# Scan stage of a hybrid encoder: a pair of heads' products in the middle of the next slot, and the low parts of the weights on GpSimd

## The chip, the cores and the metric

One core of one Trainium2 chip runs the whole computation. Its engines are TensorE (PE; matmuls into PSUM, here the eight "banks"), VectorE (DVE), ScalarE (ACT), GpSimd (POOL, which works on SBUF only here) and SyncE (SP, which issues the loads of the weights). Each engine works through its own instructions in order; they wait for each other by semaphores. The metric is the device time of one execution in microseconds (us).

## What is computed

Two layers (DEPTH = 2) over a sequence of 512 positions and a width of 1024:

```python
for i in range(DEPTH):
    h = rmsnorm(x, norm1_g[i])
    u = h @ w_in[i]
    q, k, v, z, xbc, dt_raw, sc_b, sc_c, sc_x = jnp.split(u, split_at, axis=-1)
    a_out = attention_mixer(q, k, v, q_norm_g[i], k_norm_g[i], rel_table)
    s_out = ssd_mixer(z, xbc, dt_raw, ...)
    c_out = short_conv_mixer(sc_b, sc_c, sc_x, sc_conv_w[i], sc_conv_b[i])
    x = x + jnp.concatenate([a_out, s_out, c_out], axis=-1) @ w_out[i]
    x = x + conv_ffn(rmsnorm(x, norm2_g[i]), ffn_w_up[i], ...)
```

The part around the change is `ssd_mixer`: 16 heads in 2 groups, each scanned forward and backward in 4 chunks of 128 positions. For a head, with `cb` the products C x B of a chunk, masked by direction, and `a_cs` the running sums of dt*a:

```python
decay = jnp.exp(jnp.where(lower, seg, -jnp.inf))          # seg: differences of a_cs
y_diag = jnp.einsum('bclsge,bcsgep->bclgep', cb[..., None] * decay, X)
y_off = jnp.einsum('bclgn,bcgepn->bclgep', Cc, s_in) * jnp.exp(a_cs)[..., None]
y = y_fwd + y_bwd + d_skip * xs
y = y * silu(z); y = y * rsqrt(mean(y * y) + EPS); y = y * norm_g
```

All matrices are float32, and the output is float32.

## The kernel before

**Products in three parts.** Every large product is made of float32r halves: `products` (lines 1076 to 1080) multiplies high x high, high x low and low x high and adds them in one bank. A weight tile of 1024 rows x 128 columns ([128, 1024] in SBUF) is one "chunk" of the list CHUNKS. SP loads it into one of two buffers W (line 306, after the low part of the chunk two before, `w_lo`), ACT copies it to WHI (`w_high`, line 451, once the products of the chunk two before are done, `w_used`), and the low part WLO = W - WHI is made by POOL (`w_low`, line 359) in all stages but the scan stage, and by DVE (`low_after`, line 745) in the scan stage. The product of a chunk waits for its `w_lo`. Two chunks are in flight, so in the slot of chunk n the engines prepare chunk n + 2.

**Slots.** SLOTS (line 69) are the 28 chunks from the short convolution to the first half of the output product: 12 of the short convolution ("sc"), 8 of z, 8 of the output ("o1"). Called slots 0 to 27 here. TensorE does the 24 products of a slot's tile (`tile`, or `output_first` for "o1") and, beside them, the work of the scan. All five engines' programs are loops over the slots, written out by hand; the order of the instructions of an engine is the order in its loop. Which part stands in which slot comes from three tables: GROUP_AT = (2, 14) starts the two groups, ROWS_AT gives head h the slot GROUP_AT + 3 + h % 8 (5 to 12, and 17 to 24), PAIR_AT gives the pair of heads 2t and 2t + 1 a slot (7, 9, 11, 13 and 19, 21, 23, 25).

**A head** passes through the engines thus:

- TensorE, in the middle of the slot: `row_sums` (line 1239), two products, into banks 2 and 3. It waits for the head before to have been read (`seg_read`, and ACT's `ea_done`).
- DVE `seg` (lines 820 and 823): subtracts the columns' sums and limits the result, into one of three buffers (two in E, one in SQ).
- ACT: exponential of the row sums (line 604, EA), then of the buffer (line 607), and behind them in the same slot the high part of the next weights (`high_after`).
- DVE `weigh` (line 827): times the masked products CB. In the slot it stands behind `seg` and the eviction of the slot's tile. The low part of the weights stands behind `weigh`.
- POOL `add_directions` (line 389): adds the two directions (`gs_done`).

**A pair** t: TensorE, at the end of its slot, `from_states` (line 1265, 12 products, waits for DVE to have read the pair before, `y_read`) and `within` (line 1252, 16 products, waits for `gs_done` of both heads). DVE `combine` (lines 831, 838, 839), at the end of its slot's part: reads both, adds the forward half to XC. POOL `add_backward` (line 393) adds the other half, and later `gate` (line 398) multiplies with silu(z). DVE's eviction of a z tile (line 1004) of the second half waits for a gate (`y_comb`), because it writes over the z tile that the gate reads. After slot 27 POOL's `sum_squares(1)` (lines 372, 374) gives the sum for the second group's norm, which TensorE's `scan_sum(1)` (line 1120) takes behind the first output tile of the next stage ("o2").

**POOL's loop over the slots** has, in this order: the low part of the short convolution's product (line 414), `scale_states` (line 384), `add_directions`, `add_backward`, gates, and in slot 23 `sum_squares(0)`.

Of the kernel before, what the change touches and what calls it, by code (L numbers as in the profile page):

```python
# [103 lines left out]

GROUP_AT = (2, 14)
ROWS_AT = {GROUP_AT[h // 8] + 3 + h % 8: h for h in range(SSD_HEADS)}
PAIR_AT = {GROUP_AT[t // 4] + 5 + 2 * (t % 4): t for t in range(SSD_HEADS // 2)}


NORMS = ("norm1", "ssd0", "ssd1", "norm2")  # L110
# [24 lines left out]
def build_trunk(nc, a):  # L135
# [218 lines left out]
    def _(pool):  # L354
# [6 lines left out]
        def low_after(kind, i):  # L361

            n = now[0] * NCH + POS[kind, i] + 2
            if (kind, i) == ("o2", 0):
                pool.wait_ge(w_lo.handle, n)
            if n < DEPTH * NCH:
                w_low(n)

# [33 lines left out]
        for layer in range(DEPTH):  # L402
            now[0] = layer
            for pos in range(POS["sc", 0]):
                low_after(*CHUNKS[pos])
                if layer == 0 and CHUNKS[pos] == ("qk", 2):
                    pool.wait_ge(bias_row.handle, 2)
                    g.dma_start(scratch[:, :, :], rm["bias_row"][:, :].unsqueeze(1).to_broadcast([HEADS, COPIES, REL]))\
                        .then_inc(bias_stored.handle, 16)
            for s, (kind, i) in enumerate(SLOTS):  # L410
                if kind == "sc" and i % 3 == 2:
                    t = i // 3
                    pool.wait_ge(*sc_hi.at(t + 1))
                    g.tensor_tensor(rm["ml_sc"][:, t, :], SCP[:, :], rm["mh_sc"][:, t, :].bitcast(F32), ALU.subtract)\
                        .then_inc(sc_lo.handle, 1)
                for grp in range(SSD_GROUPS):
                    if 0 <= s - GROUP_AT[grp] < 3:
                        for j in range(2):
                            scale_states(6 * grp + 2 * (s - GROUP_AT[grp]) + j)
                if s in ROWS_AT:  # L420
                    add_directions(ROWS_AT[s])
                if s in PAIR_AT:
                    add_backward(PAIR_AT[s])
                if s in (16, 17):
                    gate(2 * (s - 16))
                    gate(2 * (s - 16) + 1)
                if s in (20, 22, 24):
                    gate(s // 2 - 6)
                if s == 25:
                    gate(7)  # L430
                if s == 23:
                    sum_squares(0)
            sum_squares(1)
            for m in range(KT):
                low_after("o2", m)
            for j in range(2 * FF_T):
                low_after("up", j)
                if j % 2 == 1:
                    t = j // 2
                    pool.wait_ge(*ff_hi.at(t + 1))  # L440
                    g.tensor_tensor(FLO[:, t, :], FP[:, :], FHI[:, t, :].bitcast(F32), ALU.subtract).then_inc(ff_lo.handle, 1)  # L441
            for i in range(DOWN_C * KT):
                low_after("dn", i)
# [259 lines left out]
    def _(dve):  # L703
# [33 lines left out]
            v.scalar_tensor_tensor(mixed("l", 8 + t), XC[:, t, :], par(PA_SNG + t), mixed("h", 8 + t).bitcast(F32),  # L737
                                   ALU.mult, ALU.subtract).then_inc(y_lo.handle, 1)

        def low_after(kind, i):  # L740

            n = now[0] * NCH + POS[kind, i] + 2
            dve.wait_ge(w_hi.handle, n + 1)
            dve.wait_ge(w_lo.handle, n)
            v.tensor_tensor(WLO[:, n % 2, :], W[:, n % 2, :], WHI[:, n % 2, :].bitcast(F32), ALU.subtract).then_inc(w_lo.handle, 1)  # L745

        def root_ready(name):
            dve.wait_ge(*root_done.at(NORMS.index(name) + 1))

# [113 lines left out]
        for layer in range(DEPTH):  # L863
# [77 lines left out]
            for s, (kind, i) in enumerate(SLOTS):  # L941
# [10 lines left out]
                    dve.sem_inc(cs_col.handle, 1)  # L952
                if s in ROWS_AT:
                    seg(ROWS_AT[s])
                for grp in range(SSD_GROUPS):
                    if s == GROUP_AT[grp] + 1:
                        mask_products(grp)
                    if 0 <= s - GROUP_AT[grp] - 1 < 3:
                        for j in range(2):
                            state_in(6 * grp + 2 * (s - GROUP_AT[grp] - 1) + j)  # L960
# [23 lines left out]
                    v.tensor_tensor(X[:, i, :], bank(b), X[:, i, :], ALU.add).then_inc(evac[b].handle, 1)  # L984
                if s in ROWS_AT:
                    weigh(ROWS_AT[s])
                low_after(kind, i)
                if s in PAIR_AT:
                    combine(PAIR_AT[s])
                if kind == "sc" and i % 3 == 1:  # L990
                    t = i // 3
# [75 lines left out]
    def _(pe):  # L1067
# [32 lines left out]
            if k == KT - 1:  # L1100
                ins.then_inc(w_used.handle, 1)

        def tile(kind, i, width=P, head=None):

            for k in range(KT):
                if k == KT // 2 and head is not None:
                    row_sums(head)
                block_of(kind, i, k, width)

        def norm_sum(norm):  # L1110
# [155 lines left out]
                             start=True, stop=True)  # L1266
            ins.then_inc(yo_mm.handle, 1)

        def output_first(m, head):

            s, b = weights("o1", m), tile_bank("o1", m)
            for k in range(KT):
                if k == KT // 2 and head is not None:
                    row_sums(head)
                at = slice(P * k, P * k + P)
                ins = products(bank(b), WHI[:, s, at], WLO[:, s, at], mixed("h", k), mixed("l", k), k == 0, k == KT - 1)
            ins.then_inc(w_used.handle, 1)
# [14 lines left out]
        for layer in range(DEPTH):  # L1292
# [47 lines left out]

            for s, (kind, i) in enumerate(SLOTS):
                if kind == "o1":
                    output_first(i, ROWS_AT.get(s))
                else:
                    tile(kind, i, head=ROWS_AT.get(s))
                if s == 0:
                    pv(PAIRS - 1)
                    cumulate()
# [5 lines left out]
                for grp in range(SSD_GROUPS):  # L1354
# [4 lines left out]
                    if 0 <= s - GROUP_AT[grp] - 1 < 3:  # L1359
                        for j in range(2):  # L1360
                            chunk_state(6 * grp + 2 * (s - GROUP_AT[grp] - 1) + j)
                if s in PAIR_AT:
                    from_states(PAIR_AT[s])
                    within(PAIR_AT[s])
                if s == 26:
# [125 lines left out]
```

## Time and profile before

| | us |
|---|---|
| median of 3 runs (lowest to highest) | 1684.43 (1684.07 to 1684.91) |
| the profiled execution's own time | 1689.05 |
| its span, first to last instruction | 1687.2 |

| engine | busy us | share of the span |
|---|---|---|
| TensorE matmul | 1649.8 | 98% |
| TensorE weight load | 1306.7 | 77% |
| DVE | 1003.6 | 59% |
| ACT | 679.4 | 40% |
| POOL | 723.3 | 43% |

The granted TensorE clock is 0.997 of full speed. The scan stage of layer 0 lies at about 212 to 431 us, that of layer 1 at about 1046 to 1266 us; in the 40 equal slices of the span (42 us each) DVE is at 7 to 9 tenths there and TensorE at 9. By line, the chain that ended last runs 71% through lines 1078 to 1080 (the three products), 3% through line 745, 1% through line 820. The page's group of line 359 (POOL's low part) has 202 instructions with 490.4 us, that of line 745 (DVE's) 56 with 78.0 us.

How to read it: a row of the timeline gives an instruction's start, its length and, in brackets, how long its engine had been idle and which instruction ended that. The length of an instruction of DVE or POOL is from its start to its end, whatever it waited for inside the engine. A TensorE product is shown with its whole latency (0.39 us and more) though the next starts 0.23 us later.

### The profile page before, as it was taken

How to read it: one execution, taken by the hardware profiler on the slowest of the kernel's cores; microseconds unless marked ns; L12 is line 12 of the kernel's file. 1: busy time of each engine (PE TensorE's matmuls, PEld its weight loads, DVE VectorE, ACT ScalarE, POOL GpSimd, SP SyncE). 2: the span in 40 equal slices, each digit the busy share in tenths (PEclk: the TensorE clock that was granted, in tenths of full speed). 3: DMA queues.
4: the chain of work that ended last, by engine and by line, in shares of the span. 5: the costliest groups of instructions: out<-in, count | busy, mean ns of one | idle time of the engine just before them, and what ended most of it. 6: DMA issues, size and time to landing. Idle time of an engine off the chain costs nothing.

```text
span 1687.2 us, 20176 instructions
## 1 busy us (share of the span) xinstructions
PE 1649.8 (98%) x7876; PEld 1306.7 (77%) x7876; DVE 1003.6 (59%) x1387; ACT 679.4 (40%) x932; POOL 723.3 (43%) x355
## 2 busy tenths in 40 slices
PE   7999999998999999999999999999989999999999
PEld 5777777777778888888877777777777788888887
DVE  5589859778774555422236898596787654545100
ACT  5445553344443333322244555433543433333221
POOL 3432224345445555554444222243454455555443
PEclk9999999999999999999999999999999999999999
DMA  5532111212223232222224221122112223222223
GB/s 167 136 90 81 53 63 63 76 63 76 75 88 100 88 100 91 98 91 94 93 86 124 85 73 64 63 65 73 63 63 91 94 91 100 88 100 89 93 100 106
DMA packets 43230, 147.32 MB, mean 87 GB/s; under 512 B 5152, under 2 KB 5920, under 8 KB 43136
## 3 DMA queue, kind: packets, MB, share of 16 engines
q1 hardware_dynamic: 42752, 145.28, 26.6%
q0 software_dynamic: 384, 0.75, 0.4%
q8 instruction: 63, 1.03, 0.3%
q14 instruction: 31, 0.25, 0.1%
HBM read 143.17 MB, written 2.85 MB: 87 GB/s over the span
## 4 chain that ended last, share of the span: by engine, by line
PE 80%; DVE 10%; issue 4%; ACT 3%; POOL 2%; DMA 1%; SPq 0%; DVEq 0%; ACTq 0%; POOLq 0%
PE banks L1078 24%; PE banks L1080 23%; PE banks L1079 23%; DVE sb_w_lo L745 3%; PE banks L1170 2%; PE banks L1149 2%; PE banks L1158 2%; DVE sb_e L820 1%; ACT sb_exp_cs L604 1%; PE banks L1225 1%; PE banks L1129 1%; DVE sb_t_normed L838 1%; ACT sb_e L607 1%; DVE sb_sc_acc L995 1%; POOL sb_sq_ssd L372 1%
## 5 line engine op out<-in xcount | busy, mean ns | idle before, releaser
L359 POOL TENSOR_TENSOR sb_w_lo<-sb_w_raw,sb_w_hi 128x1024 fp32r<-128x1024 f32 x202 | 490.4, 2428 | 632.3 <-ACT sb_w_hi L451 632.3
L1078 PE MATMUL banks<-sb_h_hi,sb_w_hi 128*128 128x512 f32 x1360 | 559.1, 411 | 16.1 <-POOL sb_w_lo L359 10.8
L451 ACT ACTIVATE sb_w_hi<-sb_w_raw 128x1024 fp32r<-128x1024 f32 x258 | 272.3, 1057 | 674.4 <-PE banks L1080 668.1
L1080 PE MATMUL banks<-sb_h_hi,sb_w_lo 128*128 128x512 f32 x1360 | 538.2, 396 | 0.0
L1079 PE MATMUL banks<-sb_h_lo,sb_w_hi 128*128 128x512 f32 x1360 | 538.1, 396 | 0.0
L1078 PEld LDWEIGHTS banks<-sb_h_hi,sb_w_hi 128*128 128x128 f32 x1360 | 257.2, 189 | 100.0 <-issue 35.9
L1079 PEld LDWEIGHTS banks<-sb_h_lo,sb_w_hi 128*128 128x128 f32 x1360 | 257.4, 189 | 61.7 <-issue 6.9
L1080 PEld LDWEIGHTS banks<-sb_h_hi,sb_w_lo 128*128 128x128 f32 x1360 | 257.1, 189 | 59.7
L1043 DVE TENSOR_TENSOR banks<-banks,sb_rstd 128x512 f32<-128x512 f32 x88 | 61.5, 699 | 144.1 <-PE banks L1080 135.7
L1079 PE MATMUL banks<-sb_ff_lo,sb_w_hi 128*128 128x512 f32 x352 | 139.0, 395 | 0.0
L1080 PE MATMUL banks<-sb_ff_hi,sb_w_lo 128*128 128x512 f32 x352 | 139.0, 395 | 0.0
L1078 PE MATMUL banks<-sb_ff_hi,sb_w_hi 128*128 128x512 f32 x352 | 139.0, 395 | 0.0
L1058 DVE TENSOR_TENSOR sb_x_stream<-banks,sb_x_stream 128x512 f32<-128x512 f32 x16 | 11.1, 692 | 199.2 <-PE banks L1080 199.2
L745 DVE TENSOR_TENSOR sb_w_lo<-sb_w_raw,sb_w_hi 128x1024 fp32r<-128x1024 f32 x56 | 78.0, 1392 | 23.4 <-ACT sb_w_hi L451 23.4
L604 ACT ACTIVATE sb_exp_cs<-banks 64x768 f32<-64x768 f32 x32 | 25.8, 807 | 143.9 <-DVE sb_e L820 113.0
L441 POOL TENSOR_TENSOR sb_ff_lo<-sb_ff_prod,sb_ff_hi 128x512 fp32r<-128x512 f32 x44 | 57.0, 1295 | 51.4 <-DVE sb_ff_hi L1054 51.4
L389 POOL TENSOR_TENSOR sb_e<-sb_e 128x512 f32<-128x512 f32 x24 | 51.4, 2142 | 63.6 <-DVE sb_e L827 63.6
L1078 PEld LDWEIGHTS banks<-sb_ff_hi,sb_w_hi 128*128 128x128 f32 x352 | 66.4, 189 | 15.5
L1079 PEld LDWEIGHTS banks<-sb_ff_lo,sb_w_hi 128*128 128x128 f32 x352 | 66.4, 189 | 15.4
L1080 PEld LDWEIGHTS banks<-sb_ff_hi,sb_w_lo 128*128 128x128 f32 x352 | 66.4, 189 | 15.3
L768 DVE SCALAR_TENSOR_TENSOR sb_xc<-banks,sb_params,sb_xc 128x509 f32<-128x509 f32 (+2 forms) x96 | 71.9, 749 | 4.5 <-ACT sb_xc L508 1.7
L514 ACT ACTIVATE sb_probs<-sb_scores,sb_neg_max 128x512 f32<-128x512 f32 x64 | 45.7, 716 | 57.3 <-DVE sb_neg_max L794 57.3
(199 smaller groups left out, 2321.1 us busy)
## 6 DMA issues: line engine op xcount, KB each, us to landing
sb_w_raw<-w_in SPq DMA_DIRECT2D x88, 512.0 KB, 3.4
sb_w_raw<-w_up SPq DMA_DIRECT2D x88, 512.0 KB, 3.3
sb_w_raw<-w_out SPq DMA_DIRECT2D x32, 512.0 KB, 3.4
sb_w_raw<-w_down SPq DMA_DIRECT2D x32, 512.0 KB, 3.4
sb_bias_t<-bias_rows SPq DMA_DIRECT2D x16, 448.0 KB, 5.7
sb_w_raw<-w_down SPq DMA_DIRECT2D x16, 384.0 KB, 3.0
sb_x_stream<-x_t SPq DMA_DIRECT2D x4, 512.0 KB, 6.3
out_t<-sb_x_stream SPq DMA_DIRECT2D x8, 256.0 KB, 3.9
```

The costliest lines, as they stand in the source:

```text
L359: g.tensor_tensor(WLO[:, n % 2, :], W[:, n % 2, :], WHI[:, n % 2, :].bitcast(F32), ALU.subtract).then_inc(w_lo.handle, 1)
L389: g.tensor_tensor(head_e(h)[:, 0, :], head_e(h)[:, 0, :], head_e(h)[:, 1, :], ALU.add).then_inc(gs_done.handle, 1)
L441: g.tensor_tensor(FLO[:, t, :], FP[:, :], FHI[:, t, :].bitcast(F32), ALU.subtract).then_inc(ff_lo.handle, 1)
L451: sc.activation(WHI[:, n % 2, :], W[:, n % 2, :], ACT.Copy).then_inc(w_hi.handle, 1)
L514: sc.activation(PR[:, u % 4, :], S[:, u % 2, :], ACT.Exp, bias=NEGMAX[:, u % 4:u % 4 + 1], scale=-1.0, accum_out=DEN[:, u % 4:u % 4 + 1]). ...
L604: sc.activation(EA[half, (h // 2) % 2, :, :].rearrange("p d l -> p (d l)"), BANK[half, 2:4, :].rearrange("p b s -> p (b s)")[:, P:P + 768] ...
L745: v.tensor_tensor(WLO[:, n % 2, :], W[:, n % 2, :], WHI[:, n % 2, :].bitcast(F32), ALU.subtract).then_inc(w_lo.handle, 1)
L768: ins = v.scalar_tensor_tensor(acc[:, lo:hi], src[:, lo + o:hi + o], par(PA_CONV7 + 8 * n + t), acc[:, lo:hi], ALU.mult, ALU.add)
L1043: v.tensor_tensor(bank(b), bank(b), RSTD, ALU.mult).then_inc(up_scaled.handle, 1)
L1078: mm(out, whi, hhi, start=start, stop=False)
L1079: mm(out, whi, hlo, start=False, stop=False)
L1080: return mm(out, wlo, hhi, start=False, stop=stop)
```

## The change

It has two parts.

**Pairs.** PAIR_AT becomes GROUP_AT + 6, 8, 10 and 11: slots 8, 10, 12, 13 and 20, 22, 24, 25. Of each four, the first three pairs' `from_states` and `within` stand in the middle of the slot's tile, ahead of that slot's `row_sums` (new function `between`); the fourth stays at the end of its slot. DVE's `combine` of the first three moves up, behind `seg` and ahead of the tile's eviction and `weigh`. POOL's `add_backward` follows PAIR_AT.

**Low parts.** DVE's `low_after` goes; POOL makes the 28 low parts of the stage too, as the first thing in each slot, ahead of line 414, `scale_states`, `add_directions`, `add_backward` and the gates. POOL's wait for DVE's last low part, at ("o2", 0), goes.

```diff
-PAIR_AT = {GROUP_AT[t // 4] + 5 + 2 * (t % 4): t for t in range(SSD_HEADS // 2)}
+PAIR_AT = {GROUP_AT[t // 4] + 6 + 2 * (t % 4) - (t % 4 == 3): t for t in range(SSD_HEADS // 2)}
 ...
 # POOL
             n = now[0] * NCH + POS[kind, i] + 2
-            if (kind, i) == ("o2", 0):
-                pool.wait_ge(w_lo.handle, n)
             if n < DEPTH * NCH:
                 w_low(n)
 ...
             for s, (kind, i) in enumerate(SLOTS):
+                low_after(kind, i)
                 if kind == "sc" and i % 3 == 2:
 ...
 # DVE
-        def low_after(kind, i):
-
-            n = now[0] * NCH + POS[kind, i] + 2
-            dve.wait_ge(w_hi.handle, n + 1)
-            dve.wait_ge(w_lo.handle, n)
-            v.tensor_tensor(WLO[:, n % 2, :], W[:, n % 2, :], WHI[:, n % 2, :].bitcast(F32), ALU.subtract).then_inc(w_lo.handle, 1)
 ...
                 if s in ROWS_AT:
                     seg(ROWS_AT[s])
+                if s in PAIR_AT and PAIR_AT[s] % 4 < 3:
+                    combine(PAIR_AT[s])
 ...
                 if s in ROWS_AT:
                     weigh(ROWS_AT[s])
-                low_after(kind, i)
-                if s in PAIR_AT:
+                if s in PAIR_AT and PAIR_AT[s] % 4 == 3:
                     combine(PAIR_AT[s])
 ...
 # TensorE
-        def tile(kind, i, width=P, head=None):
+        def between(s):
+
+            if s in PAIR_AT and PAIR_AT[s] % 4 < 3:
+                from_states(PAIR_AT[s])
+                within(PAIR_AT[s])
+            if s in ROWS_AT:
+                row_sums(ROWS_AT[s])
+
+        def tile(kind, i, width=P, slot=None):
 
             for k in range(KT):
-                if k == KT // 2 and head is not None:
-                    row_sums(head)
+                if k == KT // 2 and slot is not None:
+                    between(slot)
                 block_of(kind, i, k, width)
 ...
-                if s in PAIR_AT:
+                if s in PAIR_AT and PAIR_AT[s] % 4 == 3:
                     from_states(PAIR_AT[s])
                     within(PAIR_AT[s])
```

`output_first` takes the slot in the same way.

## Rows read from the trace of the kernel before

**Rows 1.** Timeline, TensorE, layer 0's scan stage: start us, us, engine, line, what, [idle before <-releaser]

```profile
267.17 0.50 PE L1078 MATMUL banks<-sb_h_hi,sb_w_hi 128*128 128x512 f32 x1 [0.88 <-DVE sb_w_lo L745]
...
290.75 0.32 PE L1252 MATMUL banks<-sb_squares,sb_x_tok 128*64 128x128 f32 x1 [1.31 <-POOL sb_e L389]
...
321.52 1.09 PE L1252 MATMUL banks<-sb_e,sb_x_tok 128*64 128x128 f32 x16 [1.82 <-POOL sb_e L389]
...
383.07 0.50 PE L1078 MATMUL banks<-sb_mh_at,sb_w_hi 128*128 128x512 f32 x1 [0.19 <-DVE sb_w_lo L745]
...
394.15 0.73 PE L1239 MATMUL banks<-sb_cs,sb_selectors 128*128 128x512 f32 x2 [1.98 <-ACT sb_exp_cs L604]
...
416.14 1.67 PE L1252 MATMUL banks<-sb_e,sb_x_tok 128*64 128x128 f32 x16 [2.96 <-POOL sb_e L389]
...
437.37 1.13 PE L1120 MATMUL banks<-sb_sq_ssd,sb_constants 128*128 128x512 f32 x2 [0.77 <-POOL sb_sq_ssd L374]
```

**Rows 2.** Busy time by engine, columns: us, PE busy (x), PEld, DVE, ACT, POOL, PEclk, DMA share, GB/s

```profile
244.00:424.00 180.00, 170.87 (x858) 135.82 (x857) 146.34 (x169) 70.90 (x79) 78.78 (x47) 0.99 0.21 68
```

**Rows 3.** Timeline, DVE and POOL side by side (columns as in rows 1)

```profile
456.40 2.40 POOL L359 TENSOR_TENSOR sb_w_lo<-sb_w_raw,sb_w_hi 128x1024 fp32r<-128x1024 f32 x1 [2.99 <-ACT sb_w_hi L451]
...
456.60 2.76 DVE L1025 TENSOR_TENSOR sb_x_stream<-sb_x_stream,sb_t_normed 128x512 f32<-128x512 f32 x1
...
408.54 2.39 POOL L372 TENSOR_TENSOR sb_sq_ssd<-sb_sq_ssd 128x1024 f32<-128x1024 f32 x1
...
408.87 2.61 DVE L823 TENSOR_SCALAR sb_e<-sb_e 128x1024 f32<-128x1024 f32 x1
...
286.13 1.22 DVE L827 TENSOR_TENSOR sb_e<-sb_e,sb_cb 128x1024 f32<-128x1024 f32 x1
...
286.30 2.19 POOL L414 TENSOR_TENSOR sb_ml_sc<-sb_sc_prod,sb_mh_sc 128x512 fp32r<-128x512 f32 x1 [4.41 <-DVE sb_mh_sc L981]
...
287.27 2.31 DVE L745 TENSOR_TENSOR sb_w_lo<-sb_w_raw,sb_w_hi 128x1024 fp32r<-128x1024 f32 x1
...
358.19 1.22 DVE L820 TENSOR_TENSOR sb_e<-banks,sb_small 128x1024 f32<-128x1024 f32 x1
...
358.79 1.29 POOL L398 TENSOR_TENSOR sb_xc<-sb_xc,sb_z 128x512 f32<-128x512 f32 x1
```

**Rows 4.** One line's instructions: count, ns min/median/max, first and last start, form

```profile
L359 POOL TENSOR_TENSOR sb_w_lo<-sb_w_raw,sb_w_hi x202: 2343/2403/3075, 7.6 to 1675.4; 128x1024 fp32r<-128x1024 f32 x101
...
L745 DVE TENSOR_TENSOR sb_w_lo<-sb_w_raw,sb_w_hi x56: 1214/1220/2323, 224.6 to 1268.0; 128x1024 fp32r<-128x1024 f32 x56
...
L389 POOL TENSOR_TENSOR sb_e<-sb_e x24: 1295/2212/2282, 266.0 to 1249.8; 128x512 f32<-128x512 f32 x24
...
L823 DVE TENSOR_SCALAR sb_e<-sb_e x24: 693/694/2614, 258.6 to 1244.8; 128x1024 f32<-128x1024 f32 x24
...
L995 DVE SCALAR_TENSOR_TENSOR sb_sc_acc<-sb_sc_cx,sb_params,sb_sc_acc x16: 744/752/1784, 234.0 to 1138.9; 128x511 f32<-128x511 f32 x16
...
L1025 DVE TENSOR_TENSOR sb_x_stream<-sb_x_stream,sb_t_normed x32: 691/693/2759, 434.7 to 1315.1; 128x512 f32<-128x512 f32 x32
```

**Rows 5.** Timeline, TensorE and ACT, slots 19 to 22 of layer 0

```profile
365.73 1.50 PE L1265 MATMUL banks<-sb_bc,sb_s_in 128*128 128x128 f32 x12
...
368.19 0.50 PE L1078 MATMUL banks<-sb_mh_at,sb_w_hi 128*128 128x512 f32 x1
...
376.18 1.28 ACT L612 ACT_TABLE_LOAD   x1
...
380.70 1.06 ACT L451 ACTIVATE sb_w_hi<-sb_w_raw 128x1024 fp32r<-128x1024 f32 x1
```

**Rows 6.** Timeline, ACT and POOL, before the second scan sum

```profile
431.05 1.06 ACT L451 ACTIVATE sb_w_hi<-sb_w_raw 128x1024 fp32r<-128x1024 f32 x1 [1.81 <-PE banks L1080]
...
435.71 1.60 POOL L374 TENSOR_TENSOR sb_sq_ssd<-sb_sq_ssd 128x512 f32<-128x512 f32 x1
```

**Rows 7.** DMA issues: count, KB each, median us to landing

```profile
sb_w_raw<-w_out SPq DMA_DIRECT2D x32, 512.0 KB, 3.4
```

More of the change, by code:

```diff
@@ L1267, in from_states, with output_first @@
             ins.then_inc(yo_mm.handle, 1)
-        def output_first(m, head):
+        def output_first(m, slot):
             s, b = weights("o1", m), tile_bank("o1", m)
             for k in range(KT):
-                if k == KT // 2 and head is not None:
-                    row_sums(head)
+                if k == KT // 2:
+                    between(slot)
                 at = slice(P * k, P * k + P)
@@ L1342, in _ @@
                 if kind == "o1":
-                    output_first(i, ROWS_AT.get(s))
+                    output_first(i, s)
                 else:
-                    tile(kind, i, head=ROWS_AT.get(s))
+                    tile(kind, i, slot=s)
                 if s == 0:
```

## The prediction

> **What bounds the kernel now.** I read the page's busy shares first: TensorE (PE) is busy for 98% of the span, so only its waits and its work can move the time. Then its waits in layer 0's scan stage, which the change rewrites. The timeline says where they fall and who ends them: POOL's sum of the directions (L389), ACT's exponential of the sums (L604), DVE's low part of a weight tile (L745), POOL's tree of squares (L374) [rows 1]. Call the tiles of SLOTS slots 0 to 27. A plain slot is 24 products of 0.232 us, 5.57 us; one with a head's row sums 6.04; one that also has a pair's products (2.46, from 365.73 to 368.19 [rows 5], and a slower start behind them) 8.58. The idle times are 0.9 (low part, before slot 7), 1.3 (slot 9), 1.8 (13), 0.2 (22), 2.0 (23), 3.0 (25) and 0.8 (second scan sum), 9.9 together; counted from one slot's start to the next, with the slow restart behind each wait, it is 11.8 us a layer. Layer 1 repeats it. So 24 us is the most that better order can give. Behind all these waits stands DVE: in 244 to 424 us it is busy 146 of 180 us, POOL 79 [rows 2].
>
> **What decides: the path into SBUF that DVE and POOL share.** In the output stage POOL's low part starts at 456.40 and takes 2.40; DVE's L1025, normally 0.69, starts at 456.60 and takes 2.76: it ends 0.7 after POOL does. At 408.54 the same happens to L823 (2.61 for 0.69), which has one SBUF input. The other way round, at 286.13 DVE's L827 runs 1.22, POOL's L414 behind it takes 2.19, and DVE's next, L745, waits for that and takes 2.31: each holds the path for its whole instruction, the one that asked first goes next. An instruction of DVE that reads a bank is not held up: L820 at 358.19 takes 1.22 under POOL's L398 from 358.79 [rows 3]. So POOL's L389, whose median is 2.21, is really some 1.2 (its shortest is 1.295) and spends the rest behind L745 [rows 4].
>
> **The parts and their prices.**
> Low parts (28 a layer) leave DVE: L745 takes 1.22 undisturbed, so DVE is relieved of 28 x 1.22 = 34 us a layer. They come to POOL at 2.40 each (L359 median), 67 us a layer onto an engine that has time for it: 79 of 180 busy becomes some 135, less about 15 for L389 and L414 that no longer queue behind L745 [rows 2, 4]. What is not free is the path. For two slots with one pair (6.04 + 8.58 = 14.6 us) its users are, before: DVE 2 x (0.69 L823 + 1.22 L827 + 1.22 L745) + 0.56 L839 = 6.8; POOL 2 x 1.2 L389 + 1.0 L393 + 1.3 L398 = 4.7; 11.5, 79%. After: DVE 4.4, POOL 2 x 2.4 + 4.7 = 9.5; 13.9, 95%. In the short-convolution slots L995 (twice 0.75) and L981 (0.43) come once in three slots and add 1.3, and L414 (1.1) takes L398's place: 15.0, over 100% [rows 3, 4]. (0.56, 1.0 and 0.43 are the shortest of L839, L393 and L981 in the same view as rows 4.) DVE and POOL work in order and wait on each other within a slot, so a path at 95% must cost waits.
>
> Where they land I get by carrying the clocks of the queues forward slot by slot, with these durations and that rule for the path. Done for the kernel before, as a check, it returns waits of 0.9, 0.3 (slot 8's row sums, not in the rows), 1.5, 2.0, 0.4, 2.4, 3.6, 0.4 in the order above and a small 0.3 at slot 13's start: 11.8. For the changed kernel, layer 0:
> - Slots 4 to 7. The high part for slot 6 ends at 251.9, POOL holds the path to 254.3, and DVE's L858, which ran at 252.36, now goes at 254.3. DVE is 2 us late, saves 1.2 of L745, and is late again by POOL's L414 and L389 ahead of head 1's L823. L827 follows that head's exponential, then the low part for slot 8 takes 2.4 and ends at 274.4 where TensorE is ready at 272.5: **1.9**. But the 0.9 before slot 7 is gone, since that low part no longer waits for L827 and L414.
> - Slots 10 to 13: the same chain (seg, POOL's hold, exponential, high part, 2.4) gives 0.6 at slot 11, 1.8 at slot 13. `within` waits 1.1 for L389 at the end of slot 13 (2.0 before). The 1.5 of pair 1 goes: its `within` now comes at 293.3 in the middle of slot 10, and head 3's sum is ready at 292.8.
> - Slots 16 to 19: the gates (L398) now stand behind a low part, so Z's eviction and with it the bank come late: 0.9.
> - Slots 20 to 25: low parts 1.1 (slot 20), 2.2 (22), 0.9 (24), 0.8 (25). The 2.2 can be followed alone. Pair 4's products (2.46: 365.73 to 368.19) now precede head 11's row sums in slot 20, which end 2.88 + 2.46 + 0.62 = 5.96 into it. Then L820 1.22, L823 0.73, L607 1.06, Silu with its two table loads 4.52 (376.18 to 380.70), L451 1.06, L359 2.40: 16.9, against 6.04 + 8.58 = 14.62 until slot 22 [rows 4, 5]. Head 13's wait (2.4) goes, since pair 5's reading, which L604 needed first, no longer stands between.
> - Slot 25: pair 7 stays at the end, but pair 6 now stands in slot 24, so `from_states` waits 1.7 for its reading, and `within` 3.3 for L389: 5.0 for 3.6.
> - Second scan sum: the low parts of slots 26 and 27 now stand ahead of `sum_squares(1)` on POOL. High part 431.05 + 1.06, low 2.40, L372 2.39, L374 1.6: 438.5, for 437.3 before [rows 1, 3, 6]. By the stepping 1.6 for 0.4.
> Sum after: 1.9 + 0.6 + 1.8 + 1.1 + 0.9 + 1.1 + 2.2 + 0.9 + 0.8 + 5.0 + 1.6 = 17.9, less 11.8: about 6 a layer. With every duration moved by up to 5% and the comparison repeated, the middle is 5.4 and eight in ten lie within 2.3 to 8.8. I take 5.4, **11 us for two layers**.
>
> Small parts. Fewer changes of kind on TensorE: six pairs a layer now adjoin row sums. A row-sum slot costs 6.04 = 24 x 0.232 + 0.47, its two products and no more, so I take nothing; at most 0.1 each, 1.2 us in all, as a gain. SP's loads wait for low parts (`w_lo`): at worst a low part ends when its slot starts; the load lands 3.4 later, and the high part waits for the slot's end, 5.57 later [rows 7]. That cover of 2.2 holds. The wait for `w_lo` that went from ("o2", 0) was satisfied by order anyway: nothing. The moved `combine` issues the same four instructions; behind it on DVE stand the tile's eviction and `weigh`, which the stepping holds. One bound has no row: whether a low part of POOL in these slots is slowed by something else. Its longest anywhere is 3.08 (median 2.40); at 2.6 throughout the stepping gives 9.7 a layer, 19 in all; if it found the path always free, -8 a layer.
>
> The Trainium skill ("Perfetto Trace Analysis", Optimizing Scalar/DVE Operations) says that since the two engines share an SBUF port, moving operations between them might not help. By it the sum would be 0 and the time 1684; by the rows it is neither 0 nor all loss, because DVE's reads of banks do run beside POOL [rows 3]. It speaks for the third rival.
>
> **Rivals.**
> 1. It works as drawn: POOL's low parts fall under DVE's bank reads (L820, L831, L838 and the evictions, about 5.5 us in two slots) and DVE's lead removes the waits. Without any hold of the path the stepping leaves only slot 22 (2.2) and the second scan sum (1.6) of 11.8: 8 a layer, 1668. For it: POOL has the time, TensorE's 6 us waits for L389 are what the edit aims at. Against: the holds of [rows 3]. It decides if POOL's holds cost DVE less than half of the 34 us of relief; the stepping has them grow from 14 to 38 us a layer, which eats 24. A half of it, -4 a layer, gives 1676.
> 2. POOL becomes the pacer: low parts take 2.6 or more among DVE's holds, `add_directions` and the gates slip, and pair products wait in mid-slot. 9 to 10 a layer: 1703. For: 95% of the path. Against: L359's mean is 2.43.
> 3. Gains and losses cancel: the hold of L858 in slot 4 falls otherwise, DVE keeps its lead, and slots 8, 11 and 13 don't wait (1.9 + 0.6 + 1.8 = 4.3 of the 5.4 a layer): 2 us in all, 1686. For: which engine asks first there is a matter of 0.5 us. Against: other tenths then put the same hold elsewhere, as the moved durations showed.
>
> **From this to the numbers.** The profiled execution took 1689.05 (span 1687.2), 4.6 over the median of 1684.43; the 11 us are read from it and added to the median: 1695. Chances: forecast (up 4 to 17) 0.54, rival 1 0.20, rival 2 0.13, rival 3 0.13. Within 0.2%, 3.4 us, is about what can't be told from no change. Faster 0.21, same 0.14, slower 0.65. Range 1677 to 1705: it leaves out the full form of rival 1 and the tail of rival 2. The likeliest case's own range is 1688 to 1702.
>
> **What would show it.** Right: TensorE's waits name L359 POOL as releaser of L1078 in both scan stages, some 2 us ahead of slots 8, 13 and 22; L823, L827, L858 and L995 have means well above 0.69, 1.22, 0.69 and 0.75; L389 falls from 2.2 towards 1.3; the second scan sum waits about 2 us. The waits of L1252 in slot 9 and L1239 in slot 23 are gone in any case. Wrong: no such waits of L1078, with L823 and L827 at their old lengths; then DVE's relief came through and the time is under 1680. Over 1702 with L359 above 2.6 is rival 2.

## The result and the profile after

The changed kernel takes 1701.7 us (median of four runs, 1699.0 to 1703.7), the kernel before 1684.7 on the same chip: a ratio of 1.0093, 95% interval 1.0080 to 1.0105. It is slower by 17 us; the forecast was 1695, 11 slower. The profiled execution of the changed kernel took 1699.0, that of before 1689.1, so the pair of traces holds 9.9 us of the difference.

The page of the changed kernel begins:

```profile
span 1697.1 us, 20118 instructions
PE 1652.9 (97%) x7876; PEld 1306.1 (77%) x7876; DVE 990.5 (58%) x1331; ACT 680.8 (40%) x932; POOL 834.2 (49%) x411
L359 POOL TENSOR_TENSOR sb_w_lo<-sb_w_raw,sb_w_hi 128x1024 fp32r<-128x1024 f32 x258 | 630.2, 2443 | 784.5 <-ACT sb_w_hi L450 784.5
```

DVE has lost 56 instructions and only 13.1 us of busy time (1003.6 before); the group that left it, in the page of before:

```profile
L745 DVE TENSOR_TENSOR sb_w_lo<-sb_w_raw,sb_w_hi 128x1024 fp32r<-128x1024 f32 x56 | 78.0, 1392 | 23.4 <-ACT sb_w_hi L451 23.4
```

The 56 low parts took 78.0 us of DVE. So 65 of these 78 came back as longer instructions of DVE's that remain. That is the first reading that matters: a busy time counts the waiting for the path too, and 140 us of new work on POOL (L359: 630.2 for 490.4) made DVE's other work 65 us longer. POOL's own busy time rose by 111 only, because its other instructions, L389 above all, no longer wait behind DVE's low part.

In the window of [rows 2] (us, busy PE, PEld, DVE, ACT, POOL, then granted clock, DMA share, GB/s) POOL is at 119 us, DVE at 136:

```profile
244.00:424.00 180.00, 168.71 (x845) 133.25 (x844) 136.10 (x143) 69.68 (x76) 119.23 (x68) 0.99 0.19 65
```

TensorE's waits in layer 0's scan stage, which answer to [rows 1] (the timeline; start us, us, engine, line, what, idle before and its releaser; L1071 is L1078 of before, L1253 is L1252, L1121 is L1120):

```profile
273.99 0.50 PE L1071 MATMUL banks<-sb_h_hi,sb_w_hi 128*128 128x512 f32 x1 [1.82 <-POOL sb_w_lo L359]
...
312.89 0.50 PE L1071 MATMUL banks<-sb_h_hi,sb_w_hi 128*128 128x512 f32 x1 [0.71 <-POOL sb_w_lo L359]
...
320.96 1.09 PE L1253 MATMUL banks<-sb_e,sb_x_tok 128*64 128x128 f32 x16 [0.89 <-POOL sb_e L387]
...
360.55 0.47 PE L1071 MATMUL banks<-sb_h_hi,sb_w_hi 128*128 128x512 f32 x1 [1.24 <-DVE sb_z L997]
...
367.61 0.50 PE L1071 MATMUL banks<-sb_mh_at,sb_w_hi 128*128 128x512 f32 x1 [0.78 <-POOL sb_w_lo L359]
...
384.95 0.70 PE L1071 MATMUL banks<-sb_mh_at,sb_w_hi 128*128 128x512 f32 x1 [2.44 <-POOL sb_w_lo L359]
...
416.02 1.58 PE L1266 MATMUL banks<-sb_bc,sb_s_in 128*128 128x128 f32 x12 [0.43 <-DVE sb_xc L831]
...
420.57 1.09 PE L1253 MATMUL banks<-sb_e,sb_x_tok 128*64 128x128 f32 x16 [2.98 <-POOL sb_e L387]
...
441.51 1.12 PE L1121 MATMUL banks<-sb_sq_ssd,sb_constants 128*128 128x512 f32 x2 [2.07 <-POOL sb_sq_ssd L372]
```

They sum to 13.4 us for 9.9 before (idle time alone, without the slow start behind a wait). The waits of slots 7, 9 and 23 are gone, and the low parts that POOL makes now end four waits of L1071: in slots 8, 13, 20 and 22. Layer 1 shows the same list within 0.05. TensorE's products are all there in both, so the new order costs these waits and what follows a wait (below).

How POOL's low part holds DVE, from the timeline of DVE and POOL side by side, slot 4 and slot 25 (columns as above):

```profile
251.78 2.40 POOL L359 TENSOR_TENSOR sb_w_lo<-sb_w_raw,sb_w_hi 128x1024 fp32r<-128x1024 f32 x1 [3.36 <-ACT sb_w_hi L450]
252.19 2.54 DVE L850 TENSOR_TENSOR sb_t_normed<-sb_s_in,sb_decays 128x512 f32<-128x512 f32 x1
...
415.56 2.53 POOL L359 TENSOR_TENSOR sb_w_lo<-sb_w_raw,sb_w_hi 128x1024 fp32r<-128x1024 f32 x1 [0.96 <-ACT sb_w_hi L450]
416.40 2.78 DVE L819 TENSOR_TENSOR sb_e<-sb_e,sb_cb 128x1024 f32<-128x1024 f32 x1
```

The instruction of 0.68 (L850) takes 2.54, that of 1.22 (L819) takes 2.78. The first ends 0.55 after POOL does, the second 1.09: each a little less than its own undisturbed length, as if it had begun its work only when POOL was through. The groups by line (count, busy time, mean ns of one, idle before) give the same over both layers:

```profile
L815 DVE TENSOR_SCALAR sb_e<-sb_e 128x1024 f32<-128x1024 f32 x24 | 31.9, 1330 | 0.8
L819 DVE TENSOR_TENSOR sb_e<-sb_e,sb_cb 128x1024 f32<-128x1024 f32 x24 | 40.4, 1685 | 6.5 <-ACT sb_e L606 6.5
L850 DVE TENSOR_TENSOR sb_t_normed<-sb_s_in,sb_decays 128x512 f32<-128x512 f32 x16 | 16.6, 1037 | 0.0
L387 POOL TENSOR_TENSOR sb_e<-sb_e 128x512 f32<-128x512 f32 x24 | 36.3, 1511 | 7.0 <-DVE sb_e L819 7.0
```

Their means before were 896 (L823), 1223 (L827), 774 (L858) and 2142 (L389).

**What the prediction did not have: TensorE's clock.** Windows of 5 us of the changed kernel, with the same columns:

```profile
385.00:390.00 5.00, 5.00 (x18) 4.05 (x19) 4.43 (x5) 2.66 (x3) 4.18 (x3) 0.66 0.33 108
1225.00:1230.00 5.00, 5.00 (x30) 4.21 (x30) 3.58 (x5) 3.94 (x5) 3.95 (x4) 0.68 0.24 94
```

The first begins where the wait of 2.44 ahead of slot 22 ends. The products there:

```profile
385.45 0.63 PE L1072 MATMUL banks<-sb_ml_at,sb_w_hi 128*128 128x512 f32 x1
...
388.01 0.62 PE L1072 MATMUL banks<-sb_ml_at,sb_w_hi 128*128 128x512 f32 x1
388.43 0.43 PE L1073 MATMUL banks<-sb_mh_at,sb_w_lo 128*128 128x512 f32 x1
388.70 0.40 PE L1071 MATMUL banks<-sb_mh_at,sb_w_hi 128*128 128x512 f32 x1
...
395.21 0.40 PE L1071 MATMUL banks<-sb_mh_at,sb_w_hi 128*128 128x512 f32 x1
```

They start every 0.43 us for some three microseconds and every 0.23 after that: the lower of the clock's two levels (1.2 GHz), then the upper (2.4 GHz). The slot lasts 395.21 - 384.95 = 10.26. The kernel before falls too, behind its own longest wait (the 2.96 of [rows 1]):

```profile
415.00:420.00 5.00, 3.86 (x22) 3.10 (x23) 4.19 (x6) 0.00 (x0) 3.29 (x2) 0.66 0.65 208
```

A wait does not always bring it: behind the 2.98 in slot 25 of layer 0 the changed kernel kept its clock, behind the 2.97 of layer 1 it did not. Over the scan stages the profiled execution of before has three such falls (behind 1.82 and twice 2.96), that of the changed kernel four (slot 22 in both layers, slot 25 and the second scan sum in layer 1). In the scan stages of all fourteen traces each fall follows a wait of 1.8 us or more, and several waits of that length are followed by none.

### The profile page after: what moved, and what is told of

Its sections match the earlier page's. It is cut to its first block, busy times and chain, and to the rows that moved or that the text cites. A ratio compares the mean times of both kernels' runs of the same rounds, so it can differ in the third digit from the quotient of the medians.

```text
span 1697.1 us, 20118 instructions
## 1 busy us (share of the span) xinstructions
PE 1652.9 (97%) x7876; PEld 1306.1 (77%) x7876; DVE 990.5 (58%) x1331; ACT 680.8 (40%) x932; POOL 834.2 (49%) x411
## 4 chain that ended last, share of the span: by engine, by line
PE 81%; DVE 9%; issue 5%; POOL 3%; ACT 2%; DMA 0%; SPq 0%; DVEq 0%; POOLq 0%; ACTq 0%
PE banks L1071 24%; PE banks L1072 24%; PE banks L1073 24%; PE banks L1171 2%; PE banks L1150 2%; PE banks L1159 2%; DVE sb_e L812 1%; POOL sb_w_lo L359 1%; DVE sb_e L815 1%; DVE sb_e L819 1%; ACT sb_w_hi L450 1%; PE banks L1130 1%; PE banks L1253 1%; DVE sb_t_normed L850 1%; POOL sb_squares L382 1%
## 5 line engine op out<-in xcount | busy, mean ns | idle before, releaser
L359 POOL TENSOR_TENSOR sb_w_lo<-sb_w_raw,sb_w_hi 128x1024 fp32r<-128x1024 f32 x258 | 630.2, 2443 | 784.5 <-ACT sb_w_hi L450 784.5
L1071 PE MATMUL banks<-sb_h_hi,sb_w_hi 128*128 128x512 f32 x1360 | 557.7, 410 | 21.1 <-POOL sb_w_lo L359 14.9
L1071 PEld LDWEIGHTS banks<-sb_h_hi,sb_w_hi 128*128 128x128 f32 x1360 | 256.4, 189 | 105.9 <-issue 38.3
L1071 PE MATMUL banks<-sb_ff_hi,sb_w_hi 128*128 128x512 f32 x352 | 138.9, 395 | 0.0
L1071 PEld LDWEIGHTS banks<-sb_ff_hi,sb_w_hi 128*128 128x128 f32 x352 | 66.3, 188 | 15.6
L1038 DVE SCALAR_TENSOR_TENSOR sb_ff_val<-banks,sb_params,sb_ff_val 128x511 f32<-128x511 f32 x44 | 33.0, 750 | 46.2 <-ACT sb_ff_val L683 46.2
L1038 DVE SCALAR_TENSOR_TENSOR sb_ff_gate<-banks,sb_params,sb_ff_gate 128x511 f32<-128x511 f32 x44 | 33.0, 750 | 45.8 <-ACT sb_ff_gate L683 45.8
```

The lines of the kernel that those rows point to most:

```text
L359: g.tensor_tensor(WLO[:, n % 2, :], W[:, n % 2, :], WHI[:, n % 2, :].bitcast(F32), ALU.subtract).then_inc(w_lo.handle, 1)
L1038: step(v.scalar_tensor_tensor(acc[:, 1:SEQ], BANK[:, b, 0:SEQ - 1], par(col), acc[:, 1:SEQ], ALU.mult, ALU.add))
L1071: mm(out, whi, hhi, start=start, stop=False)
```

## The experiments

Three questions: is it POOL's hold of the path that costs; how much of the relief of DVE is left when the hold is shorter or better placed; and are the falls of the clock the part that the order of the queues does not explain?

**The pairs moved, nothing else.** The low parts stay on DVE behind `weigh` (and POOL's wait for them comes back). Comments in the code below are added here.

```
+POOL_LOW = ()
-                low_after(kind, i)              # POOL, at the slot's start
+                if s in POOL_LOW:
+                    low_after(kind, i)
...
+                if s not in POOL_LOW:           # DVE, behind weigh
+                    low_after(kind, i)
```

> Pairs moved as in the changed kernel, but all 28 low parts of the scan stage stay on DVE, behind weigh. Theory 1 (the path into SBUF that DVE and POOL share): the pairs' move is worth nothing by itself; the queues carried forward give +0.3 us a layer, so 1685 +- 3, with TensorE's waits at low parts before slots 10 (2.4) and 22 (2.1) in place of slots 9 and 23. Theory 2 (the order: the pair in mid-slot delays the row sums and with them the slot): most of the loss stays, 1697 to 1702.

1686.3 for 1686.4 of the kernel before: ratio 1.0001 (0.9991 to 1.0011). Waits of TensorE in 240 to 450 us (us in total, times, longest):

```profile
PE banks L1084 <- DVE sb_w_lo L748: 4.9, 3, 2.1
PE banks L1266 <- POOL sb_e L390: 2.8, 2, 2.3
```

The waits for the sum of the directions shrink, those for DVE's low part take their place. The pairs' half of the change is worth nothing alone.

**The low parts moved, nothing else.** They are on POOL at the slot's start as in the change, and the pairs stay at the ends of slots.

> Low parts on POOL at the start of each slot as in the changed kernel, pairs at the end of slots 7, 9, 11, 13 as before. Theory 1: worse than the changed kernel, since within now comes before POOL has added the directions: +8.9 us a layer, 1702 and, with the clock's dips behind long waits, up to 1710; waits at L1252 of 2 to 3 us in slots 7, 9, 21. Theory 2 (order of the pairs is the loss): the low parts on POOL alone are a gain or nothing, 1675 to 1685.

1706.9: ratio 1.0119 (1.0105 to 1.0133), 20 us slower than before.

```profile
PE banks L1243 <- POOL sb_e L387: 12.1, 6, 3.8
```

The whole loss is in this half: on POOL the low part now stands ahead of the sum of the directions, and a pair at the end of its slot waits for that six times (3.8 us at worst). Moving the pairs takes 3 to 4 us of it back (20.4 to 17.0, though the intervals of their ratios just touch), as they have half a slot more to spare.

**Shorter holds.** POOL makes 512, then 16, of the 1024 columns of each low part in these slots; the rest of the low part is left out, and nothing else changes.

```
-                low_after(kind, i)
+                low_after(kind, i, 512)      # and 16 in the second kernel
```

> The changed kernel, but POOL makes only columns 0 to 511 of each of the 28 low parts of the scan stage (the other half of WLO keeps old values). Each low part then takes about 1.25 us and holds the path as long as DVE's did. Theory 1: the loss turns into a gain, -8.3 us a layer against before, 1668 +- 4. Theory 3 (POOL's place in the order, behind the end of the slot, is what hurts, not the length of its holds): still slower than before, 1690 or more.

> The changed kernel, but POOL makes only 16 of the 1024 columns of each of the 28 low parts of the scan stage (the rest of WLO keeps old values). DVE keeps its full relief of 34 us a layer, POOL holds the path for almost nothing. Theory 1 (path): all waits go but some 0.7 us at slot 25: -11.2 us a layer, 1662 +- 4. Theory 3 (POOL's place in the order): no better than the half lows, 1670.

With 512 columns 1670.5, ratio 0.9903 (0.9890 to 0.9917). With 16 columns 1666.2, ratio 0.9883 (0.9869 to 0.9896). All of TensorE's waits in layer 0's stage with 512 columns:

```profile
PE banks L1071 <- POOL sb_w_lo L359: 1.3, 1, 1.3
PE banks L1121 <- POOL sb_sq_ssd L372: 1.0, 1, 1.0
PE banks L1253 <- POOL sb_e L387: 0.9, 1, 0.9
```

The second is 0.2 us outside what was expected (1662 +- 4). So the relief of DVE, with the pairs moved, is worth 19 us, and half of POOL's work per slot still leaves 16 of it. It is the second 512 columns that cost, 31 us against 4 for the first; some 6 of the 31 are falls of the clock in the changed kernel, which these two, with no wait over 1.3 us in this stage, do not have. This says nothing of *how* POOL's work costs, by its own length or by the hold. The next run shows what holds alone do.

**The hold alone.** To the kernel with the pairs moved, one operation of POOL's is added in each slot from 2 on, on tiles of its own; nobody waits for its result. DVE still makes the low parts.

```
+                if s >= 2:
+                    pool.wait_ge(w_hi.handle, now[0] * NCH + POS[kind, i] + 3)
...
+                    g.tensor_tensor(SM[:, 1:4, :], CON[:, 0:6, :]..., CON[:, 1:7, :]..., ALU.subtract)...
```

> The kernel with the pairs moved and all low parts on DVE, and in each slot from 2 on one more instruction on POOL at the place of the low part, behind the same wait, that subtracts 768 columns of the constants into dead storage: nobody waits for its result, it only holds the path for 1.8 us and delays what stands behind it on POOL. Theory 1: slower by 20 to 28 us a layer than the pairs alone (DVE has not been relieved here), 1727 to 1742. If holds were harmless and only the low part's later end hurt, 1686 to 1690.

1743.5 (1740.6 to 1746.0), ratio 1.0339 (1.0318 to 1.0359). The low parts on DVE and the added group, then what TensorE waits for in 240 to 450 us:

```profile
L753 DVE TENSOR_TENSOR sb_w_lo<-sb_w_raw,sb_w_hi 128x1024 fp32r<-128x1024 f32 x56 | 102.7, 1833 | 18.0 <-ACT sb_w_hi L459 18.0
...
L418 POOL TENSOR_TENSOR sb_small<-sb_constants 128x768 f32<-128x768 f32 x52 | 107.6, 2069 | 200.1 <-ACT sb_w_hi L459 200.1
```

```profile
PE banks L1089 <- DVE sb_w_lo L753: 15.4, 7, 4.1
PE banks L1271 <- POOL sb_e L391: 6.6, 2, 3.3
PE banks L1089 <- DVE sb_z L1015: 3.4, 3, 2.4
```

Fifty-two operations of 2.07 us that produce nothing that is used cost 57 us, 1.1 each. DVE issues the same instructions as with the pairs alone, and its busy time goes from 1011.5 to 1062.5 us; its low part takes 1833 ns in the mean for 1422, and TensorE's waits for DVE's tiles (L753, L1015) go from 4.9 us to 18.8 in this stage. Not all of the 57 is the path's: POOL's queue is longer too (6.6 us for L391, for 2.8), DVE waits for POOL in places, and the profiled execution has ten falls of the clock in the scan stages where the pairs alone had none, at most 20 us by the clocks of its windows (an estimate). The time is just above what was expected (1727 to 1742). How the loss of the changed kernel divides between the holds and the low part's own 2.40 us on POOL (for 1.22 on DVE) no run shows. By the prediction's own working the waits at slot 22 and at the second scan sum come from the low part's length and place and would be there without any hold.

**Low parts put by slot.** First the twelve slots in which the stepping found POOL's low part cheapest (0, 2, 3, 5, 6, 8 to 11, 13, 14, 22), the rest on DVE; and a kernel that gives DVE back only the last two, 26 and 27.

> The changed kernel's pairs; low parts on POOL in slots 0, 2, 3, 5, 6, 8 to 11, 13, 14, 22 and on DVE in the other 16, chosen by carrying the queues forward. Theory 1: -3.8 us a layer, 1677, and a little less if fewer long waits also mean fewer dips of the granted clock; waits left at slots 13 (1.3), 22 (2.0), 25 (3.9). If the path were not what decides, the mix would lie between e1 and the changed kernel, 1690 or more.

> The changed kernel with the low parts of slots 26 and 27 back on DVE, so that sum_squares(1) no longer stands behind them on POOL. The queues carried forward give 1.2 us a layer less than the changed kernel, the wait at the second scan sum 0.4 to 0.8 us as before in place of 2.1. With no wait of over 2 us there, no fall of the granted clock behind it either: 1702 - 2.4 - up to 3, so 1697 to 1699. If the clock's falls are unrelated to waits, 1699 to 1700.

1678.7 for the first, ratio 0.9950 (0.9937 to 0.9964). 1697.4 for the second, ratio 1.0068 (1.0055 to 1.0081), 4 us under the changed kernel, though the two intervals just touch. The wait of the second scan sum goes from 2.1 to 0.8 in both layers, and no fall follows it. With the falls taken out (how, is shown in the next section) its trace gives 1694.2 for the changed kernel's 1696.0, so the two low parts themselves cost some 2 us and the rest is falls.

Then each slot got the place that the stepping liked best, and so did the pairs: 0, 1, 2, 5 and 6 in mid-slot, 3, 4 and 7 at the end of slots 13, 19 and 25.

```
+MID = (0, 1, 2, 5, 6)
+LOW_BY = 'PPDPDPPDPPEPDQEPEDPPDEEQDDPE'
```

P is POOL at the slot's start, Q POOL behind the sum of the directions, D DVE behind `weigh`, E DVE ahead of it. The string has 14 on POOL and 14 on DVE; the expectation counts 13 and 15.

> A better order, searched by carrying the queues forward: pairs 0, 1, 2, 5, 6 in mid-slot, 3, 4, 7 at the end of slots 13, 19, 25; low parts on POOL in 13 slots (two of them behind add_directions) and on DVE in 15 (six of them ahead of weigh). -5.7 us a layer: 1673, 3 to 4 us under the mixed kernel; waits left at slots 22 (1.5), 25 (1.9 and 1.1), none over 2 us, so few falls of the clock.

1673.2 (1672.8 to 1674.0), ratio 0.9925 (0.9913 to 0.9938): some 12 us faster than the kernel before, 28 faster than the changed one, the best that computes all of the low parts. What is left in layer 0's stage:

```profile
PE banks L1089 <- POOL sb_w_lo L361: 1.7, 2, 1.1
PE banks L1089 <- DVE sb_w_lo L751: 1.3, 1, 1.3
PE banks L1139 <- POOL sb_sq_ssd L376: 0.8, 1, 0.8
PE banks L1271 <- POOL sb_e L391: 0.6, 1, 0.6
```

No wait is over 1.3, and the granted clock of its whole span was 1.000 in all its runs.

**Filling the waits, to keep the clock up.** Three products of constants with ones (nobody reads the result; 2.7 us of TensorE; a row counts each as two) go into four waits of the changed kernel: ahead of `within` of pairs 3 and 7, at the end of slot 21, and ahead of the second scan sum. The same goes into the kernel before.

```
+                if s == 21:
+                    warm(7)          # 3 products, 128x512, fp32, into a bank that is free
```

> The changed kernel, with three products more of the constants (about 2 us of TensorE, into a bank that is overwritten next) ahead of four long waits of each layer: within of pairs 3 and 7, the start of slot 22, the second scan sum. They fill idle time; the waits end when they ended. Theory A (the granted clock falls to 1.2 GHz for some 2.8 us behind a long wait, and that costs 1.4 us each time): no falls are left there, 4 to 7 us less than the changed kernel, 1695 to 1698. Theory B (the falls have nothing to do with the waits): same as the changed kernel or slower by what of the extra products isn't hidden (up to 1 us each at pair 3 and the second scan sum), 1700 to 1706.

> The kernel before, filled in the same way ahead of within of pairs 3 and 7 and of the second scan sum (its longest waits are 3.0, 1.8 and 0.8 us; three products take about 2). Theory A: no falls behind slots 13 and 25, so up to 2.8 us less in the executions that had them, less 0.2 to 1.2 us where the extra products outlast the wait: 1683 to 1686 with a smaller spread than before's 1684.4 to 1691. Theory B: slower by 2 to 3 us, the same spread.

1702.4 for the changed kernel, ratio 1.0091 (1.0074 to 1.0107), no change; 1690.6 for before, ratio 1.0022 (1.0012 to 1.0031), slower, with a spread of 3.9 us for 7.3. By time neither speaks for the clock. The traces do. In the scan stages each has two falls left, and all four stand behind a wait that was not filled: slot 8's 1.8 in the changed kernel (windows from 270 and 1115 us), slot 23's 2.0 in the kernel before (395 and 1235 us). At slot 22 of the first:

```profile
385.65 2.74 PE L1198 MATMUL banks<-sb_constants 128*128 128x512 f32 x6
...
388.27 0.51 PE L1071 MATMUL banks<-sb_mh_at,sb_w_hi 128*128 128x512 f32 x1
...
396.97 0.39 PE L1071 MATMUL banks<-sb_mh_at,sb_w_hi 128*128 128x512 f32 x1
```

The slot takes 8.70 for 10.26. But 2.7 us of filling outlasts three of the four waits (0.9, 2.4, 2.1), and in the kernel before those of 1.8 and 0.8, and gives the gain back: before's runs with a mean clock of 1.000 took 1684.1 to 1684.4, those filled 1689.6 to 1689.7, and the fillings outlast their waits by 2.8 us a layer. So the last pair: fillings that fit (one product of 0.9 us at the end of slot 7; two at the end of slot 21, ahead of `within` 7 and ahead of the second scan sum), and the changed kernel once more on the same chip.

> The changed kernel with fewer extra products, each set shorter than the wait that it fills (one product is 0.9 us): one at the end of slot 7 (wait 1.8), two at the end of slot 21 (2.4), two ahead of within of pair 7 (3.0), two ahead of the second scan sum (2.1). None of them moves the end of a wait. Theory A (falls of the granted clock behind the waits are part of the loss): clock near 1.000, 1692 to 1696, against 1699 to 1704 for the changed kernel on the same chip. Theory B (they are not): as the changed kernel, 1699 to 1704.

> The changed kernel itself, on the chip of the run beside it: 1699 to 1704 with clocks of 0.993 to 0.997, the longer the lower the clock.

Fitted: 1696.4 (1695.6 to 1697.4 in six runs), ratio 1.0056 (1.0043 to 1.0069). The changed kernel again: 1704.9 (1698.8 to 1705.3), ratio 1.0099 (1.0082 to 1.0116). From `within` of slot 25 to the second scan sum, first fitted, then the changed kernel again:

```profile
421.21 1.09 PE L1264 MATMUL banks<-sb_e,sb_x_tok 128*64 128x128 f32 x16 [1.25 <-POOL sb_e L387]
...
442.17 1.12 PE L1124 MATMUL banks<-sb_sq_ssd,sb_constants 128*128 128x512 f32 x2 [0.37 <-POOL sb_sq_ssd L372]
```

```profile
422.23 1.98 PE L1253 MATMUL banks<-sb_e,sb_x_tok 128*64 128x128 f32 x16 [2.97 <-POOL sb_e L387]
...
446.06 1.13 PE L1121 MATMUL banks<-sb_sq_ssd,sb_constants 128*128 128x512 f32 x2 [2.07 <-POOL sb_sq_ssd L372]
```

The stretch takes 20.96 and 23.83, with granted clocks of 1.00 and 0.67 in 420 to 425 us: this fall costs 2.9. Not every fall costs. Slot 22 and `from_states` of slot 25 in the fitted kernel, where slot 22 did not fall:

```profile
385.56 0.50 PE L1071 MATMUL banks<-sb_mh_at,sb_w_hi 128*128 128x512 f32 x1 [0.74 <-POOL sb_w_lo L359]
...
416.66 1.58 PE L1277 MATMUL banks<-sb_bc,sb_s_in 128*128 128x128 f32 x12 [1.28 <-DVE sb_xc L831]
```

That is 31.10 us, and 31.07 (384.95 to 416.02) in the changed kernel, whose slot 22 did fall: `from_states` waits for DVE there (1.28, and 0.43 behind the fall), so the fall in slot 22 makes later waits shorter and costs nothing. Layer 1 has 31.10 and 31.11.

Seven products a layer, 12.6 us of *added* work on TensorE, make the kernel 8.4 us faster, and the spread shrinks from 6.5 to 1.7. No queue of another engine was touched. The times are 0.4 and 0.9 us above what was expected. The mean clock of the whole span was 1.000 in all six runs with fillings, 0.992 to 0.996 in those without; in those five the time goes with it (0.996: 1698.8; 0.993: 1704.3; 0.992: 1704.9 to 1705.3). So the falls of the clock are a real part of the loss, and what differs from one execution to the next goes with them.

## Why the prediction was right, and where it was not

**Right: the mechanism.** The price was put on the path into SBUF, not on POOL's time, and the trace has it in the lines that were named: L823, L827 and L858 with means of 1.33, 1.69 and 1.04 for 0.90, 1.22 and 0.77, L389 down from 2.1 to 1.5 without DVE's low part ahead of it. The prediction had 14 us of holds a layer grow to 38 and eat 24 of 34 us of relief. Measured over both layers: 56 x 1.22 = 68 of undisturbed work left DVE, whose busy time fell by 13, so the holds grew by 55, some 28 a layer. The added operation that nobody waits for shows it as a cause, not as a coincidence.

**Right, within half a microsecond: six of the named places.** Foretold and found for layer 0: slot 8 1.9, 1.8; `within` 3 1.1, 0.9; the slot behind Z's eviction 0.9, 1.2; slot 20 1.1, 0.8; slot 22 2.2, 2.4; `within` of slot 25 3.3, 3.0. The second scan sum came at 2.1 for 1.6. The waits of slots 9 and 23 are gone as said. Slot 22's was followed from L820 to L359, and that chain held.

**Wrong places.** Slot 11 does not wait, and slot 13 waits 0.7 for 1.8. The low parts of slots 24 and 25 (0.9 and 0.8 foretold) do not wait in the profiled execution, and `from_states` of slot 25 waits 0.4 for 1.7; but there the fall of slot 22 hides them. In the fitted kernel, without that fall, slots 24 and 25 start 0.2 and 0.3 late and `from_states` waits 1.3. In all the forecast is 3.3 a layer too high at these places, where which engine asks first is a matter of tenths.

**The order of the queues: 11 us forecast, 11.7 found.** The falls can be taken out of the traces, by the same stretch with and without one. Before: three falls of 1.6, so 1689.05 - 4.7 = 1684.4, and its runs with a mean clock of 1.000 took 1684.1 to 1684.4. Changed: the two of slot 22 cost nothing, the other two 1.4 and 1.6 (20.94 us from `within` of slot 25 to the second scan sum in layer 0, 22.36 in layer 1; 415.5 from there to the end, 413.9 in the fitted kernel), so 1699.0 - 3.0 = 1696.0. The changed kernel again: 1.6 at slot 8 (40.50 us from slot 8 to slot 13, for 38.90) and 2.9 behind slot 25 in each layer, so 1704.9 - 8.9 = 1696.0. The fitted kernel, with no fall at all, took 1696.4. So this term was sized well. In part that is luck: the forecast counts waits with the slow restart behind them, and what it has too much at the places above it has too little, by some 3 us a layer (an estimate), at those that it named rightly: their idle time alone is 12.2 us, for 12.1 foretold with the restarts in.

**The term that was missing: the clock.** The working took a slow restart behind each wait as a constant and priced no fall, though the 2.96 of [rows 1] is followed by one in the trace of before. It set aside that the profiled execution lay 4.6 us over the median; those 4.6 are the three falls, 4.7. Behind waits of 1.8 to 3.0 us the clock went down to 1.2 GHz for about 3 us in some executions, at 1.4 to 1.6 us each (2.9 for the longer ones behind slot 25), where no other wait swallowed them. The changed kernel has more waits of that length (1.8, 2.4, 3.0 and 2.1 in each layer for 1.8, 2.0 and 3.0 before). Of the 17.0 us between the medians, 11.7 are then the queues and 5.3 falls: 5.7 in the changed kernel's median of 1701.7, 0.3 in before's. The forecast of 1695 is 7 short for this reason above all; the measured time lies at the edge of the likeliest case's own range (1688 to 1702), and the full range to 1705 reached further because it took in a rival that is false.

**The rivals.** The first (it works as drawn, 1668 or 1676) is false for this change, but its point of decision was the right one: cut the holds in half and the time is 1670.5. It said that without any hold only slot 22 and the second scan sum would wait, 1668. With 16 columns, which takes the low part's own length away too, it was 1666.2 with waits of 0.4, 0.3 and 0.3. The second (POOL paces, low parts of 2.6 or more, 1703) gave nearly the measured time and is false: L359's mean is 2.44, as before, and POOL is busy 119 of 180 us, as forecast (135 less 15). A time that agrees is no evidence for a mechanism; the row is. The third (it cancels, 1686) is out by its time, and its condition failed: the hold of L858 in slot 4 fell as drawn (2.54 at 252.19), and slot 8 waited. Of its three places two came as it said, slot 11 wholly (0 for 0.6) and slot 13 for the most part (0.7 for 1.8). The Trainium skill ("Perfetto Trace Analysis", Optimizing Scalar/DVE Operations) was weighed for this rival. The move did not help, as it warns that it might not, but the result is a loss and not a zero, and with half of the low parts moved (14 of 28 a layer, each to a chosen slot) it is a gain of some 12 us.

## What to carry to other kernels

An engine with idle time is no free place for work if it shares a path with the one that is relieved: count the path's users in one period of the pipeline, and price each instruction of DVE's that would start inside POOL's. What pays is to move some of the instructions, one by one, to where DVE reads banks or idles (some 12 us faster here, where moving all was 17 slower). A wait of two microseconds on TensorE can cost more than itself: no wait under 1.8 us in these scan stages was followed by a fall of the clock, and a few products that fit into the longer ones gave more than they took. And when the profiled execution is slower than the median, its trace is the place to ask why: here the 4.6 us that were set aside belonged to the missing term of the forecast.

## What the runs showed of the chip

- What POOL's low part costs does not go with its length: with 1024 columns (2.4 us) in each slot the kernel is 17 us slower than before, with 512 16 us faster, with 16 columns 19 us faster. Nearly all of the cost comes between 512 and 1024 columns; nothing between was run.
- A DVE instruction with a single SBUF input and an SBUF output (L815) is held as one with two is: 1330 ns in the mean for 693 at its shortest in [rows 4]. One that reads a bank, L812, keeps 1216 ns in the mean for 1217 before, and its like in the kernel with the added holds 1215.
- The time of a kernel with long waits spreads more: 1699 to 1705 for the changed one, 3.0 us for the one with twelve low parts on POOL (waits to 2.3), 1.2 and less for those with half or 16 columns and for the best order (none over 1.3 in layer 0's stage), 1.7 for the one with fitted fillings.
- A fall of the clock costs only where nothing later waits: in slot 22 it lengthened the slot by 1.6 us, and `from_states` of slot 25 began at the same time as without it (31.07 and 31.10 us behind the slot's start).
